# Feed-forward gate and up products over both parts of x at once, and linear attention's values and gates half by parts

## The reference, cut to what matters

```python
def _swiglu(x, w_gate, w_up, w_down):            # D_FF = 2816
    return (jax.nn.silu(x @ w_gate) * (x @ w_up)) @ w_down

def gla_mixer(x, w_in, gate_w, gate_b, norm_g, w_out):
    q, k, v, r, glr = split(x @ w_in)            # 512, 512, 1024, 1024, 32 columns
    loga = log_sigmoid(glr @ gate_w + gate_b) / 16
    o = gla_chunked(q, k, v, loga_fwd) + flip(gla_chunked(flip(q), flip(k), flip(v), loga_bwd))
    return (jax.nn.silu(r) * head_norm(o)) @ w_out
```

## Time and profile before

| what | value |
|---|---|
| median of 3 runs | 1698.14 us |
| profiled execution: span | 1695.9 us |
| its own time | span and about 2.2 us around it, taken from the median |
| PE busy | 1349.1 us (80%) |
| DVE busy | 604.9 us (36%) |
| ACT busy | 433.6 us (26%) |
| GLA from the first `project` to the end of the last | 610.3 to 681.8 us |
| feed-forward 0, from its first product | 1181.1 to about 1370 us |
| feed-forward 1, from its first product | 1499 to about 1686 us |

### The profile page before, as it was taken

One profiled execution on the slowest core, in us unless ns is written; L12 is line 12 of the kernel. 1 busy time (PEld: TensorE's weight loads), 2 busy tenths in 40 slices (PEclk: granted clock), 3 DMA queues, 4 the chain that ended last, 5 costly groups with the idle time before them and its releaser, 6 DMA issues.

```text
span 1695.9 us, 21317 instructions
## 1 busy us (share of the span) xinstructions
PE 1349.1 (80%) x8912; PEld 891.9 (53%) x8912; DVE 604.9 (36%) x1013; ACT 433.6 (26%) x704; POOL 41.5 (2%) x53
## 2 busy tenths in 40 slices
PE   9999565475475999993754647669999999999997
PEld 8785121121121675741211212126999979889996
DVE  5664000010000466630000000005655567875556
ACT  4552000000000433520000000004443455644443
POOL 2000000000000112000000000000000000000000
PEclk9999787797778999997877877789999999999999
DMA  9759999999999953699999999999555753065550
GB/s 364 219 217 400 432 430 429 431 427 433 429 431 427 394 185 124 277 403 427 432 430 430 429 429 432 429 426 391 186 169 195 247 198 114 13 240 172 197 197 25
DMA packets 130565, 536.82 MB, mean 317 GB/s; under 512 B 8148, under 2 KB 71892, under 8 KB 102716
## 3 DMA queue, kind: packets, MB, share of 16 engines
q1 hardware_dynamic: 126480, 530.08, 77.9%
q10 hardware_dynamic: 2380, 2.31, 0.9%
q0 software_dynamic: 1632, 3.38, 0.6%
HBM read 533.12 MB, written 2.62 MB: 316 GB/s over the span
## 4 chain that ended last, share of the span: by engine, by line
PE 53%; DMA 38%; DVE 5%; ACT 2%; SPq 2%; issue 1%; ACTq 0%; DVEq 0%
PE bank L2074 14%; PE bank L845 12%; DMA ring<-in_moe_w_down 11%; DMA ring<-in_moe_w_up 8%; PE bank L2092 7%; DMA arena<-in_moe_w_down 5%; DMA moe_slots<-in_moe_w_down 5%; PE bank L1389 5%; DMA xT_pair<-in_moe_w_up 5%; DMA moe_slots<-in_moe_w_up 4%; PE bank L1429 4%; PE bank L683 3%; PE bank L1723 1%; SPq L1639 1%; DVE stats L426 1%
## 5 line engine op out<-in xcount | busy, mean ns | idle before, releaser
L764 DVE TENSOR_TENSOR w_lo<-ring,w_hi 128x1024 fp32r<-128x1024 f32 x185 | 226.0, 1224 | 172.6 <-ACT w_hi L759 171.9
L1389 PE MATMUL bank<-ring,arena 128*32 128x512 f32 x960 | 218.2, 734 | 71.3 <-DMA arena<-in_moe_w_up 36.9
L759 ACT ACTIVATE w_hi<-ring 128x1024 fp32r<-128x1024 f32 x185 | 195.5, 1060 | 260.5 <-PE bank L2074 140.2
L1429 PE MATMUL bank<-ring,arena 128*32 128x512 f32 x496 | 146.1, 725 | 55.2 <-DMA ring<-in_moe_w_down 23.1
L2074 PE MATMUL bank<-xT_hi,w_lo 128*128 128x256 f32 x656 | 185.6, 283 | 0.0
L2074 PE MATMUL bank<-xT_lo,w_hi 128*128 128x256 f32 x656 | 185.6, 283 | 0.0
L2074 PE MATMUL bank<-xT_hi,w_hi 128*128 128x256 f32 x656 | 185.6, 283 | 0.0
L1553 DVE TENSOR_TENSOR arena<-arena,bank 64x512 f32<-64x512 f32 x32 | 22.1, 691 | 405.4 <-ACT arena L1490 405.4
L1389 PE MATMUL bank<-moe_slots,arena 128*32 128x512 f32 x352 | 109.4, 781 | 60.3 <-DMA ring<-in_moe_w_up 35.6
L1389 PEld LDWEIGHTS bank<-ring,arena 128*32 128x32 f32 x960 | 50.7, 130 | 154.9 <-issue 145.7
L1490 ACT ACTIVATE arena<-bank 64x512 f32<-64x512 f32 x32 | 18.8, 588 | 425.8 <-PE bank L1389 425.8
(11 more groups left out here) (334 smaller groups left out, 2427.3 us busy)
## 6 DMA issues: line engine op xcount, KB each, us to landing
ring<-in_moe_w_up SPq DMA_DIRECT2D x24, 2048.0 KB, 38.6
ring<-in_moe_w_down SPq DMA_DIRECT2D x22, 2048.0 KB, 40.0
ring<-in_moe_w_gate SPq DMA_DIRECT2D x20, 2048.0 KB, 39.8
moe_slots<-in_moe_w_gate SPq DMA_DIRECT2D x18, 2048.0 KB, 37.6
arena<-in_moe_w_up SPq DMA_DIRECT2D x14, 2048.0 KB, 37.9
arena<-in_moe_w_gate SPq DMA_DIRECT2D x12, 2048.0 KB, 38.7
ring<-in_w_gate SPq DMA_DIRECT2D x22, 1024.0 KB, 5.1
ring<-in_w_up SPq DMA_DIRECT2D x22, 1024.0 KB, 5.2
```

The costliest lines, as they stand in the source:

```text
L759: nc.scalar.activation(dst, raw, ACT.Copy).then_inc(hi_ready, 1)
L764: nc.vector.tensor_tensor(lo, raw, hi.bitcast(F32), ALU.subtract).then_inc(split_ready, 1)
L1389: last = nc.tensor.matmul(ps[B_GU[j % 2]][32 * c:32 * c + 32, :], xin[:, j, k, :], w, start=(k == 0), stop=(k == KD - 1), tile_position=(0 ...
L1429: last = nc.tensor.matmul(ps[B_DN[c]][32 * j:32 * j + 32, :], hT[:, j // 2, at:at + CAP], slot_row(ud[j], f % 2)[:, c * HALF:(c + 1) * HAL ...
```

## The change

Feed-forward: `xT_hi` and `xT_lo` become the two halves of one tensor, and one matmul of 512 columns takes `w_hi` times both; a matmul of 256 columns adds `w_lo` times `xT_hi` to the second half of the bank. So gate and up of a block each fill a whole bank, and the two halves have to be added: DVE does it by `tensor_reduce` (`gate_sum` and in `product`). Silu and product then read SBUF. The banks are now used again in every step, so PE waits for `fprod_ready`. In `gate_up_first` the up products run two slices behind the gate products. GLA: of each `project`, one weight unit stays plain and the other goes by parts (chunks 8 to 15 of `gla_mix`, which now has 24); at level 0 the keys need no exponential; the merges of levels 5, 6 and 7 are block copies on ACT. The load of the table `rel_t` counts on `par_in` in place of a semaphore of its own.

```diff
+        with nc.sbuf_tensor("xT_parts", [P, 2 * KD * SEQ], F32R) as xT_parts, \
+        xT_both = xT_parts[:, :].rearrange("p (n k t) -> p n k t", n=2, k=KD)
+        xT_hi3, xT_lo3 = xT_both[:, 0], xT_both[:, 1]
...
-        gla_mix = Mixer(gla_u[0:4] + gla_u[12:16], 2, chunk0["gla"])
+        gla_mix = Mixer(gla_u[0:4] + gla_u[5:12:2] + gla_u[12:16], 2, chunk0["gla"])
...
+            def plain_rows(n, start):
+                u, i = gla_u[4 + 2 * (n // 2)], n % 2
...
+            def split_rows(n, start):
+                m, i = n // 2, n % 2
+                for c in (8 + 2 * m, 9 + 2 * m):
+                    pe.wait_ge(split_ready, gla_mix.at + c + 1)
+                    for k2 in range(2):
+                        k = KD // 2 + c % 2 * 2 + k2
+                        for p, (wp, xp) in enumerate(PARTS):
...
-                token_major(pe, gla_u[4 + 2 * m:6 + 2 * m], i, V_BANKS[n], halves)
+                for part in parts:
+                    (plain_rows, split_rows)[part != i](n, part == 0)
...
             def level(n):
-                pe.wait_ge(kd_ready, n + 1)
+                if n:
+                    pe.wait_ge(kd_ready, n)
...
+            def block_merge(n):
+                act.wait_ge(lv_psum, n + 1)
+                act.wait_ge(lv_done, 2 * n)
+                l = LEVELS[n]
+                for i in range(NT):
+                    prod = ps[level_bank(n, i)][:, :].rearrange("p (h t) -> p h t", h=4)
+                    if l == P:
+                        ins = nc.scalar.activation(gl_A[:, i, :, (1 - i) * P:(2 - i) * P], prod, ACT.Copy)
+                    else:
+                        for r in range(P // l):
+                            rows, cols = slice(r * l, (r + 1) * l), slice((r ^ 1) * l, ((r ^ 1) + 1) * l)
+                            ins = nc.scalar.activation(gl_A[rows, i, :, i * P:(i + 1) * P][:, :, cols], prod[rows, :, cols],
+                                                       ACT.Copy)
+                    ins.then_inc(lv_done, 1)
...
             key_rows(0)
+            hi(act, 8)
             for n in range(len(LEVELS)):
-                for w in range(2):
+                for w in range(2) if n else (1,):
...
                 if n == 0:
                     key_rows(1)
+                    hi(act, 9, 10)
+                elif n <= 5:
+                    hi(act, 10 + n)
+                if n > BLOCK_LEVEL:
+                    block_merge(n - 1)
+                if n == len(LEVELS) - 1:
+                    block_merge(n)
...
-                merge(n)
+                if n < BLOCK_LEVEL:
+                    merge(n)
                 if n + 2 < len(LEVELS):
                     args(n + 2)
-            lo(dve, 8, 9)
+                if n < 5:
+                    lo(dve, 11 + n)
+            lo(dve, 16, 17)
...
             def gate_up_first(at):
-                for k in range(KD):
+                for k in range(KD + 2):
...
+                    if k >= 2:
+                        for wp in range(2 if m == 0 else 1):
+                            part(1, k - 2, wp, xT_hi3, start=(k == 2 and wp == 0))
...
-            def gate_up(s, at, blocks=(0, 1), third=None):
+            def gate_up(at, before=None, blocks=(0, 1), third=None):
                 for f in blocks:
+                    if before is not None:
+                        pe.wait_ge(fprod_ready, before + f)
                     for n in range(2):
...
-                            for p, (wp, xp) in enumerate(PARTS):
-                                last = nc.tensor.matmul(ps[2 * s + f][:, n * SEQ:(n + 1) * SEQ],
-                                                        w[wp][:, k * P:(k + 1) * P],
-                                                        (xT_hi3, xT_lo3)[xp][:, k, :],
...
+                            both = nc.tensor.matmul(gate_up_bank(f, n)[:, :], w[0][:, k * P:(k + 1) * P], xT_both[:, :, k, :],
+                                                    start=(k == 0), stop=False)
...
+                            last = nc.tensor.matmul(gate_up_half(f, n, 1), w[1][:, k * P:(k + 1) * P], xT_hi3[:, k, :],
+                                                    start=False, stop=(k == KD - 1))
...
         def ffn_scalar(act, m):
...
+            def steps(g, first_step=False):
...
+                    split_hi(act, us[0], g, gate_up_chunk(us, 0, 0), 0, at)
+                    if first_step and s == 0:
+                        silu(0, 1, m * NF + 1)
+                    split_hi(act, us[1], g, gate_up_chunk(us, 0, 1), 1, at + 1)
+                    split_hi(act, us[0], g, gate_up_chunk(us, 1, 0), 0, at + 2)
+                    silu(1 - s, 0, blocks)
+                    split_hi(act, us[1], g, gate_up_chunk(us, 1, 1), 1, at + 3)
+                    split_hi(act, ud, g, down_chunk(ud, 0), 0, at + 4)
+                    silu(1 - s, 1, blocks + 1)
+                    split_hi(act, ud, g, down_chunk(ud, 1), 1, at + 5)
...
         def ffn_vector(dve, link, m, gen):
...
+            def gate_sum(s, f, done):
+
+                dve.wait_ge(chunk_done, done)
+                nc.vector.tensor_reduce(f_silu[:, 2 * s + f, :], both_halves(f, 0), AX.X, ALU.add).then_inc(fgate_ready, 1)
+
+            def product(s, f, blocks, done):
 
                 b = 2 * s + f
+                dve.wait_ge(chunk_done, done)
+                nc.vector.tensor_reduce(f_up[:, f, :], both_halves(f, 1), AX.X, ALU.add).then_inc(fparts_ready, 1)
+                dve.wait_ge(fparts_ready, 2 * blocks + 1)
                 dve.wait_ge(fsilu_ready, blocks + 1)
-                nc.vector.tensor_tensor(f_silu[:, b, :], f_silu[:, b, :], ps[b][:, SEQ:2 * SEQ], ALU.mult).then_inc(fprod_ready, 1)
+                nc.vector.tensor_tensor(f_silu[:, b, :], f_silu[:, b, :], f_up[:, f, :], ALU.mult).then_inc(fprod_ready, 1)
...
                     split_lo(dve, gate_up_chunk(us, 0, 0), 0, at)
...
                     split_lo(dve, gate_up_chunk(us, 0, 1), 1, at + 1)
-                    hidden(s, 1, blocks)
...
                     split_lo(dve, gate_up_chunk(us, 1, 0), 0, at + 2)
...
+                    gate_sum(1 - s, 0, at + 1)
...
                     split_lo(dve, gate_up_chunk(us, 1, 1), 1, at + 3)
-                    hidden(1 - s, 0, blocks + 1)
-                    split_lo(dve, down_chunk(body[3 * s + 2], 0), 0, at + 4)
...
-                    split_lo(dve, down_chunk(body[3 * s + 2], 1), 1, at + 5)
+                    product(1 - s, 0, blocks, at + 2)
+                    parts(1 - s, 0, blocks)
+                    split_lo(dve, down_chunk(ud, 0), 0, at + 4)
+                    gate_sum(1 - s, 1, at + 3)
...
+                    split_lo(dve, down_chunk(ud, 1), 1, at + 5)
+                    product(1 - s, 1, blocks + 1, at + 4)
+                    parts(1 - s, 1, blocks + 1)
```

More of the change, by code:

```diff
@@ L1694, in gla_tensor, with project @@
             pe.wait_ge(ga_in, 8)
-            def project(n, halves=range(2)):
+            def plain_rows(n, start):
+                u, i = gla_u[4 + 2 * (n // 2)], n % 2
+                pe.wait_ge(slot_landed[u.slot], u.landed)
+                w = slot(u, KD // 2)
+                for k in range(KD // 2):
+                    last = nc.tensor.matmul(ps[V_BANKS[n]][:, :], xT3[:, k, i * P:(i + 1) * P], w[:, k, :],
+                                            start=(start and k == 0), stop=(not start and k == KD // 2 - 1))
+                if i:
+                    last.then_inc(unit_done, 2)
+            def split_rows(n, start):
[5 more added lines that the diff above has]
+                        for p, (wp, xp) in enumerate(PARTS):
+                            last = nc.tensor.matmul(ps[V_BANKS[n]][:, :], (xT_hi3, xT_lo3)[xp][:, k, i * P:(i + 1) * P],
+                                                    split_buffer(wp, gla_mix.buffer(c))[:, k2 * HALF:(k2 + 1) * HALF],
+                                                    start=(start and k == KD // 2 and p == 0),
+                                                    stop=(not start and k == KD - 1 and p == 2))
+                    if i:
+                        last.then_inc(chunk_done, 1)
+            def project(n, parts=range(2)):
                 m, i = n // 2, n % 2
@@ L2058, in gate_up_first @@
                             pe.wait_ge(xlo_ready, n_x + k // 2 + 1)
-                        last = part(n, k, 0, xT_lo3, stop=(n == 1 and k == KD - 1 and m == 0))
+                        last = part(n, k, 0, xT_lo3, low=True, stop=(k == KD - 1 and (n == 0 or m == 0)))
                     if n and m:
@@ L2105, in ffn_tensor @@
                     open_acc(i, c)
-            gate_up(0, c0, (1,), third=2)
+            gate_up(c0, blocks=(1,), third=2)
             with pe.Fori(0, 5) as g:
@@ L2116, in ffn_scalar, with silu @@
             c0 = chunk0[f"ffn{m}"]
-            def gate_up(us, g, at, blocks=(0, 1)):
-                for f in blocks:
-                    for n in range(2):
```

(9 more changed lines are left out.)

151 lines of the change are left out of this document (78 added, 73 removed).

## The result

The changed kernel takes 1715.59 us (median of 4 runs, 1714.92 to 1716.23) against 1698.41 before (median of 4 runs here, one more than in the table above; 1696.96 to 1699.26): ratio 1.0103, 95% interval 1.009 to 1.0117. It is slower by 17.2 us. Predicted were 11.9 more, 1710, in a range of 1703 to 1742. The profiled execution has a span of 1713.8 us, 17.9 above the one before.

What follows compares the result with a forecast made beforehand. Feed-forward and GLA were taken as bound by the distance between PE's matmuls. Feed-forwards +16.4, gate_up_first +0.7 and GLA -5.2 sum to +11.9 us: 1707.8 in the profile, 1710 as the median, range 1703 to 1742.

Steps and rivals of the forecast that it cites:

- The sum: Feed-forward, DVE: each added reduction of 512 elements out of PSUM takes 0.69 us, bounds 0.42 and 1.05.
- rival of slow strided reads: Feed-forward sums: scattered PSUM reads make each take 1.05 us, giving 1742 us in all; chance 15%.
- The loop: Feed-forward: gate's silu waits for DVE's sum ahead of ACT's next split, so splits come late and PE waits.
- The walk: Feed-forward step timed through PE, ACT and DVE queues: period 17.90 us against 17.11; 1710 in all, chance 70%.
- The step: Feed-forward: a steady step takes 17.90 us against 17.11, 0.79 lost in each.
- First step and end: Each feed-forward's first step takes about 18.3 us, 1.2 more; two chunks ahead save 0.16; no term for the end.
- Chunks on PE: Feed-forward gate or up chunk: 2.80 us for 2.88, 6.5 us less PE work, lost in waiting.
- gate_up_first: Start of feed-forwards: up to four more 0.12 us matmuls behind x's last part, two in feed-forward 1: +0.7 us.
- GLA: Half projects 2.76 us for 3.44, level period 7.98 for 8.65, level 7 waits 0.4; total -5.2 us, kept by the stream.
- block copies of level 5: GLA's tail, ACT: at most 0.45 us per 128-column piece; eight end at 7.4, before PE reaches level 6 at 7.98.
- break-even at a sum of 0.45: Feed-forward alone breaks even there; from the rival of cheap sums, 0.42 each, total 1690.4 us, chance 8%.
- third rival: Feed-forward: ACT or DVE hand over faster than counted, loop about 17.3 us, no change at 1698; chance 7%.

Runs made afterwards that it cites:

- run 3: Changed kernel with the 512-column product cut into two of 256 columns, sums and order unchanged: 1715.90 us against 1715.59, step 18.25 against 18.21.
- silu_late: Changed kernel with each of a step's two silus put behind the next split on ACT instead of ahead of it: 1694.87 us, step 17.11.
- three_products: Changed kernel with the 512-column product cut into two of 256 columns, sums and order unchanged: 1715.90 us.
- no_sums: Changed kernel without the four sums of a step; silu and product read only the first half of the bank: 1687.21 us, step 16.77.
- parts_late: silu_late with the second block's cast and rest behind the next step's first split on DVE, and one first-step seed scaling moved earlier: 1689.00 us.
- ffn_only: Kernel before the change with only the feed-forward half of the diff, GLA as before: 1720.82 us, ratio 1.0122 to 1.0153.
- block7: Changed kernel with GLA's merges of levels 5 and 6 back on DVE, level 7's still on ACT: 1716.14 us against 1715.59.
- runs 4 and 5: Changed kernel with each gate sum taken twice: 1741.14 us; the same with silus behind the next split: 1699.71; changed kernel without sums: 1687.21.
- grouped_late: parts_late with each chunk's eight 512-column products ahead of its eight 256-column ones instead of alternating: 1690.14 us, step 16.83.
- three_late: parts_late with the 512-column product cut into two of 256 columns: 1692.32 us, step 17.00.

## Why the prediction was right

It said slower, 1710 and 1703 to 1742, by one mechanism; 1715.6 was measured and the mechanism is the one that the runs show. Step by step:

- **The sum.** 0.69 was taken, 684 ns it is. The rival of slow strided reads falls: neighbouring elements half a bank apart are read at the pace of L1553's stride of four. The rule of the Trainium skill (Advanced Engine Details and Errata, Memory Cachelines), carried over to VectorE's reads of PSUM, does not hold here.
- **The loop.** The walk had ACT's split of chunk 4 right behind the silu, and PE waiting at chunks 4, 6 and the next 1. All three are there. Chunk 4 starts 8.76 us after chunk 1 (8.62 in the walk, which begins behind the 0.11 that the restart of chunk 1 loses), chunk 5 11.83 (11.57). PE waits at chunk 5 too, 0.30 in its weight loads (1272.94), where the walk had it just in time.
- **The step** was mis-sized: 17.90 for 18.21 measured. Two handovers on DVE were taken too short. From the start of the up sum to that of the next split there are 1.94 us (1269.73 to 1271.67), where 1.81 was counted (8.48 to 10.29). Most of it lies behind the sum: the product reads what the sum writes and starts 0.13 after its end (1269.73 + 0.68 to 1270.54), where the walk took 0.03 for every such handover. This comes twice a step, 0.26. And at the turn of the loop, every second step, DVE's next split comes 0.54 after the rest's start instead of 0.34 (0.10 per step):

```profile
1259.29 0.43 DVE L2246 TENSOR_TENSOR h_lo<-arena,h_hi 128x256 fp32r<-128x256 f32 x1
1259.83 1.23 DVE L766 TENSOR_TENSOR w_lo<-ring,w_hi 128x1024 fp32r<-128x1024 f32 x1
...
1277.66 0.43 DVE L2246 TENSOR_TENSOR h_lo<-arena,h_hi 128x256 fp32r<-128x256 f32 x1
1278.00 1.22 DVE L766 TENSOR_TENSOR w_lo<-ring,w_hi 128x1024 fp32r<-128x1024 f32 x1
```

  These give 18.26. The 0.3 in each of nine steps are 2.8 us per feed-forward, 5.5 in all, which is nearly the whole miss of the forecast, 5.6. That the other terms leave so little is in part luck: they are off both ways, as follows.
- **First step and end.** From the opening of the accumulators to the first down chunk it is 18.66 (1181.61 to 1200.27) for 18.15 before, +0.5, where +1.0 was said (1.2 less 0.16). From the first down chunk of the tenth step to the end there is +0.9 (10.09, 1364.05 to 1374.14, for 9.21), of which the prediction had nothing: the last down chunks wait for splits too.
- **Chunks on PE.** 2.83 in the steady part (1264.03 to 1266.86) for 2.80. It did not matter, as the walk said and run 3 shows.
- **`gate_up_first`.** From the first part of x to the opening of the accumulators: in feed-forward 0 6.64 before and 7.12 after, +0.5. In feed-forward 1 7.37 before and 7.61 in silu_late, three_products, no_sums and parts_late: +0.2. Together the +0.7 of the prediction. The profiled execution of the changed kernel has 8.76 there, and the reason is the clock:

```profile
1499.00:1503.00 4.00, 2.18 (x15) 1.77 (x16) 3.51 (x6) 3.47 (x8) 0.00 (x0) 1.00 1.03 418
1503.00:1506.00 3.00, 2.92 (x17) 2.71 (x16) 2.93 (x6) 1.73 (x3) 0.00 (x0) 0.64 1.06 384
1506.00:1509.00 3.00, 3.00 (x23) 3.00 (x22) 2.29 (x3) 0.00 (x0) 0.00 (x0) 0.79 0.92 324
```

  (busy by stretch, columns as in rows 2): the granted clock is 0.64 and then 0.79, so at 1.2 instead of 2.4 GHz for a part of these stretches, after PE had been busy 2.18 of 4 us. But silu_late and three_products were busy 2.19 of the same 4 us, ffn_only and parts_late 2.18, and in all four the clock stayed at 1.00; what made it fall in this execution is not shown. So 1.15 us (8.76 less 7.61) of the trace's 17.9 are the clock's and not the products'. Whether the runs without a trace had the fall too is not known; the profiled one took 1715.81, close to the median.
- **GLA.** Half projects 2.73 to 2.76 as said, the level period 7.96 (658.05 to 666.01) for 7.98 said, level 7 waits 0.51 for 0.4, the end 5.5 earlier for 5.2, and the stream behind keeps it. The block copies of level 5 are much cheaper than their bound: 268 ns each for at most 450, and end at 664.6, 1.4 ahead of level 6. No rival came true here; block7 shows that they are needed, for 1.2 us.
- **The rivals.** The break-even at a sum of 0.45 was not tried, since no cheaper form of the sum was measured. That a price far above it is fatal and one of nothing gives a gain is shown by runs 4 and 5. The third rival had the hand-overs quicker than counted; they are slower.

What the prediction did not see is how cheap the cure was. It named the order as the cost ("It is the order that costs") and had the numbers to see that the silu could stand behind the split, but it priced the change only as it is.

## What to carry to other kernels

When work is added to an engine that is busy for two thirds of the time, its price is not its duration but where it stands in a queue: walk the queues of a period once, and look for a loop that passes the added work and an operation that the bottleneck engine waits for. An operation whose result is wanted late, but which waits for another engine, must not stand ahead of one that is wanted soon: here two instructions moved by one place each were worth 20.7 us of 1715. And in the walk, count the hand-over between two dependent instructions of one engine (0.13 us here behind the sum) and the turn of a program loop (0.2): the first comes twice in each of twenty steps, the second in every other step.

## What the runs showed of the hardware that was not expected

- A chunk of eight pairs of a 512 and a 256-column product has two paces, with the same instructions and a granted clock of 1.00: 2.83 us in the changed kernel (1264.03 to 1266.86) and in silu_late (1244.13 to 1246.96), 2.77 in most steps of parts_late (1242.19 to 1244.97), which has 2.83 as well (1275.82 to 1278.65). no_sums has both too, one in one step (1225.07 to 1227.90) and the other in the next (1241.80 to 1244.58). What chooses between them stays open.
- A sum over two elements 1 KB apart in PSUM costs no more than one over neighbours in SBUF: 684 ns for 512 elements, 676 there.
- A small copy out of PSUM on ACT costs by its elements per partition and not by its partitions: 268 ns for 32 x 128 (271 for the 128 x 128 of L2506, a square), 381 for 64 x 256 (384 for the 128 x 256 of L1494), 595 for 128 x 512. The rows' 453 for 128 x 128 have a scale and a bias from SBUF; L729, with a scale from there alone, takes 404.
- At the start of feed-forward 1 the granted clock fell in two of the eleven traces with the new `gate_up_first`: in the changed kernel as shown above, and in grouped_late, which has 0.66 and 0.77 in six microseconds there and takes 8.37 us for the stretch. Seven others take 7.60 to 7.62. (grouped_late and the two left, block7 and three_late, lack the record of the first of four opening products, which makes their stretch look some 0.23 longer.) So single traces of this kernel can differ by 1.15 us for the clock alone.
